# Other staging places, and other load times, for the four split operands of the first down group

## What is computed

```
h = x + rms_norm(mixer(...), n_mix_post)
f = square(relu(rms_norm(h, n_ffn_pre) @ w_up)) @ w_down      # 1024 -> 4096 -> 1024, fp32
y = h + rms_norm(f, n_ffn_post)
```

## Time and profile before

| | us |
|---|---|
| median of 3 runs | 1588.58 |
| the profiled execution | 1588.32 |
| its span | 1586.3 |
| PE busy in it | 1531.6 |
| DVE, POOL, ACT busy | 933.8, 710.3, 507.2 |

### The profile page before, as it was taken

One profiled execution on the slowest core, in us unless ns is written; L12 is line 12 of the kernel. 1 busy time (PEld: TensorE's weight loads), 2 busy tenths in 40 slices (PEclk: granted clock), 3 DMA queues, 4 the chain that ended last, 5 costly groups with the idle time before them and its releaser, 6 DMA issues.

```text
span 1586.3 us, 27880 instructions
## 1 busy us (share of the span) xinstructions
PE 1531.6 (97%) x10928; PEld 1515.1 (96%) x10928; DVE 933.8 (59%) x1202; ACT 507.2 (32%) x701; POOL 710.3 (45%) x508
## 2 busy tenths in 40 slices
PE   6999999999999999999999999999999799999995
PEld 5999999999999998999999999999999799999995
DVE  6899959764485235211152785776566557474746
ACT  4100000242240224100112566665556333232333
POOL 3344444442244222444448344554555355454555
PEclk9999999999999999999999999999999899999998
DMA  5211121113321232111143024566658576464634
GB/s 178 94 47 47 46 61 47 40 60 106 94 94 46 85 98 73 43 46 46 47 154 93 1 88 147 188 216 239 214 187 305 183 274 214 161 214 161 214 101 161
DMA packets 99034, 194.85 MB, mean 123 GB/s; under 512 B 7920, under 2 KB 19952, under 8 KB 97024
## 3 DMA queue, kind: packets, MB, share of 16 engines
q1 hardware_dynamic: 85008, 169.98, 31.9%
q10 hardware_dynamic: 13936, 23.60, 4.6%
HBM read 137.50 MB, written 56.05 MB: 122 GB/s over the span
## 4 chain that ended last, share of the span: by engine, by line
PE 53%; DVE 3%; ACT 1%; DMA 1%; POOL 1%; issue 1%; SPq 0%; POOLq 0%; DVEq 0%; ACTq 0%
PE ps L1018 37%; PE ps L672 13%; PE ps L931 3%; DMA hq_g<-hidden_scratch 1%; DVE tx_l L427 1%; ACT mix L1356 0%; ACT fx_h L1339 0%; SPq L489 0%; POOL h_res L617 0%; DVE hq_g L2135 0%; POOLq L96 0%; POOL fac L652 0%; DVE mix L1945 0%; DVE mix L1942 0%; DVE mix L1943 0%
## 5 line engine op out<-in xcount | busy, mean ns | idle before, releaser
L583 POOL TENSOR_TENSOR w_h<-raw,zero 128x512 fp32r<-128x512 f32 x130 | 143.2, 1101 | 503.4 <-PE ps L672 381.8
L1018 PE MATMUL ps<-tx_h,w_h 128*128 128x258 f32 x960 | 272.8, 284 | 12.9 <-POOL w_l L641 12.4
L1018 PE MATMUL ps<-tx_l,w_h 128*128 128x258 f32 x960 | 272.3, 284 | 0.0
L1018 PE MATMUL ps<-tx_h,w_l 128*128 128x258 f32 x960 | 272.1, 283 | 0.0
L641 POOL TENSOR_TENSOR w_l<-raw,w_h 128x512 fp32r<-128x512 f32 x120 | 180.0, 1503 | 162.8 <-ACT w_h L1411 162.1
L672 PE MATMUL ps<-xn_h,w_h 128*128 128x344 f32 x1128 | 247.8, 326 | 2.4 <-DVE xn_l L1635 1.4
L672 PE MATMUL ps<-xn_l,w_h 128*128 128x344 f32 x1128 | 241.7, 320 | 0.0
L672 PE MATMUL ps<-xn_h,w_l 128*128 128x344 f32 x1128 | 240.8, 319 | 0.0
L1018 PE MATMUL ps<-fx_h,w_h 128*128 128x258 f32 x720 | 204.1, 283 | 0.0
L1018 PE MATMUL ps<-fx_l,w_h 128*128 128x258 f32 x720 | 203.4, 282 | 0.0
L1018 PE MATMUL ps<-fx_h,w_l 128*128 128x258 f32 x720 | 203.2, 282 | 0.0
(11 more groups left out here) (287 smaller groups left out, 2598.5 us busy)
## 6 DMA issues: line engine op xcount, KB each, us to landing
raw<-wseq_dram SPq DMA_DIRECT2D x264, 256.0 KB, 2.7
quad_scratch<-quad_h SPq DMA_DIRECT2D x16, 774.0 KB, 3.6
tx_h<-quad_scratch SPq DMA_DIRECT2D x12, 1032.0 KB, 10.4
tx_l<-hidden_scratch SPq DMA_DIRECT2D x12, 1032.0 KB, 12.8
hidden_scratch<-hq_g SPq DMA_DIRECT2D x8, 1032.0 KB, 6.9
hq_g<-hidden_scratch SPq DMA_DIRECT2D x8, 1032.0 KB, 12.3
hidden_scratch<-stg_b SPq DMA_DIRECT2D x6, 1032.0 KB, 6.9
rope<-rope_dram ACTq DMA_DIRECT2D x2, 2064.0 KB, 7.9
```

The source lines that it names most:

```text
L583: pool.tensor_tensor(hi, raw[:, s, :], zero[:, 0:1].broadcast_to([P, SLOT]), ALU.add).then_inc(w_hi, 1)
L1018: out = pe.matmul(ps[:, 2 * n + s, 0:HC], RINGS[q % RING][wa][:, kk * P:(kk + 1) * P], OPS[x][xb][:, QK * kh + kk, at_:at_ + HC], start=(i ...
```

## The change

```diff
+        op0, _ = place("op0", [P, QK, HT], F32, a_C0)
...
-        def staged_h(k):
+        def staged_h(g, k):
+            if g == 0 and k < 2:
+                return op0[:] if k == 0 else hq_d[:, 4:8, :]
+            if g == 0:
+                k -= 2
             return (stg_a, stg_b)[k][:, 0:QK, HT:T] if k < 2 else hq_g[:, 4 * k - 8:4 * k - 4, :]
...
             def load_operand(g, k):
-                if g:
+                if g == 1 and k < 2:
+                    lo_made(sp, 0, k + 2)
+                elif g > 1:
                     lo_made(sp, g - 1, k)
-                sp.dma_start(staged_h(k), uscr[g, OP_SLOT[SPLIT[k]]]).then_inc(stg_ld[k], 16)
+                sp.dma_start(staged_h(g, k), uscr[g, OP_SLOT[SPLIT[k]]]).then_inc(stg_ld[k], 16)
...
+                if v in (UPV - 5, UPV - 4):
+                    for u in (QK - 2, QK - 1):
+                        stored(sp, u)
+                    if v == UPV - 4:
+                        sp.wait_ge(hs_sq, 2 * KT)
+                        sp.wait_ge(h_sp, 16 * len(H_STORE))
+                    load_operand(0, v - (UPV - 5))
                 if v == UPV - 2:
-                    stored(sp, UNITS - 4)
-                    quads_stored(sp, UNITS - 4)
-                    load_operand(0, 0)
-                    load_operand(0, 1)
+                    for u in (QK - 2, QK - 1, UNITS - 4):
+                        stored(sp, u)
+                        quads_stored(sp, u)
+                    load_operand(0, 2)
+                    load_operand(0, 3)
                 if v >= UPV - 1 and p == 3 and v + 1 < NV:
                     for i in range(2, 5):
                         load_quads(g + 1, i)
-                        if v == UPV - 1 and i != 3:
-                            stored(sp, UNITS - 3)
-                            quads_stored(sp, UNITS - 3)
-                            load_operand(0, 2 + i // 4)
...
                 if d >= 0 and p == 1 and g + 1 < GROUPS:
...
+                    if g == 0:
+                        stored(sp, UNITS - 3)
+                        quads_stored(sp, UNITS - 3)
                     for k in range(4):
                         load_operand(g + 1, k)
```

More of the change, by code:

```diff
@@ L1430, in staged_hi @@
                 act.wait_ge(pm, step_done(UPV + QK * g - 1, SPLIT[k]))
-                quad_hi(SPLIT[k], staged_h(k)).then_inc(c_hi, 1)
+                quad_hi(SPLIT[k], staged_h(g, k)).then_inc(c_hi, 1)
             def h_square(n):
@@ L2006, in staged_lo @@
                     dve.wait_ge(c_hi, 4 * g + k + 1)
-                    quad_lo(dve, SPLIT[k], staged_h(k), slice(2 * half, 2 * half + 2)).then_inc(c_lo, 1)
+                    quad_lo(dve, SPLIT[k], staged_h(g, k), slice(2 * half, 2 * half + 2)).then_inc(c_lo, 1)
             def h_add(n):
```

## The result

The changed kernel takes 1577.64 us (median of 5 runs, 1577.53 to 1581.27) against 1588.58 us before (5 runs, 1588.06 to 1594.04). The ratio is 0.9931, with a 95% interval of 0.9918 to 0.9944: 0.7% faster. Forecast were 1576.3 us and a range of 1575.2 to 1578.8.

A forecast was written before the change was run, and what follows sets the result against it. PE, busy 97% of the span, was taken as the bound. Profiled 1588.32 minus 12.29 gave 1576.03, plus 0.26 to the median: 1576.3 us, range 1575.2 to 1578.8; this path had 79% and its own range 1575.4 to 1577.2.

The forecast's parts named there:

- The bound, and the mechanism: PE bounds; at v=14 it idles 10.6 us because step 3's weight waits behind late k=3 in ACT's queue.
- (a): At v=14 ACT finds k=2 and k=3 loaded; copies start at 1232.10 and 1233.93, the weight's high part at 1235.76.
- (b): Step 3's weight is late next: PE waits 0.47 to 1.04 us, taking POOL's median of 1.46 us.
- other sum: POOL, contending with DVE, takes 1.85 us for step 3's weight; time 0.39 us more than forecast.
- The price of the hole: Step 3 took 5.22 us behind the hole against 2.87 at full clock; the low clock cost 2.35 us.
- ceiling of 12.94: Most that can be won, in us: step 3's old end at 1253.11 minus its end without the hole, 1240.17.
- (c): Gain 12.29 us; behind step 3 nothing else waits: operand i=4 lands near 1239.2, step 6 is covered by 1.7 us.
- first rival: Direct operand i=4 still lands at 1241.6, making step 4 0.8 us late: gain 11.5, time 1577.1 us; chance 10%.
- (d): One added 1032 KB load at v=9 and one at v=10 cost 0, at most 2.7 us each.
- (e): Moved waits at v=15 and copies from other SBUF places cost 0; places bounded at 0.1 us either way.
- Clock rivals: Remaining wait at step 3 drops the clock again (1578.6 us, 5%), or PE without rest gets less clock (3%).
- slower rival: Unbroken PE run behind 1240.8 us is throttled: clock 0.963 loses the gain, 0.95 gives 1593.4 us; chance 3%.

The follow-up runs named there:

- ACT-order experiment: Kernel before the change, loads and places unaltered; at v = 14 ACT makes high parts of weights 3, 4, 5 ahead of staged copy k = 3: 1581.5 us.
- late k = 3 experiment: Changed kernel, but only k = 2 (and k = 0) leaves the load burst; k = 3 is loaded last at v = 13: 1585.73 us.
- both weights first: Changed kernel with ACT making the high parts of step 3's and 4's weights ahead of staged copies k = 2 and 3: 1576.36 us.
- weight-between experiment: Changed kernel; ACT makes step 3's weight between both staged copies, DVE the second half of k = 2's low part after emptying step 2's banks: 1576.48 us.
- k = 2 late: Changed kernel, but only k = 3 (and k = 1) leaves the burst; k = 2 is loaded at v = 13 between direct operands 2 and 3: 1577.85 us.

## Why the prediction was right, step by step

- **The bound, and the mechanism** (the weight of step 3 behind k = 3 in ACT's queue): right. The ACT-order experiment removes the hole without touching a load; the late k = 3 experiment keeps it with k = 2 gone.
- **(a) k = 3 and k = 2 no longer awaited**: right. In the old profile's time (0.92 us less) the copies start at 1232.10 and 1233.94 and the weight's high part at 1235.75, against 1232.10, 1233.93 and 1235.76.
- **(b) What is late next**: the right wait, 0.28 us too short. POOL took 1.74 us here (1.75 in the other two profiles of the program), and I took the median of 1.46. It was inside the bounds (1.28 to 1.85), but DVE was busy beside it. In the rows at this point the one that starts second pays. In the changed kernel POOL starts at 1237.37, within DVE's half of k = 2's low part (1236.75 to 1237.97), and takes 1.74 instead of 1.28, while that half takes 1.22. With both weights first POOL ends at 1238.05 and DVE's second half, started at 1237.41, takes 1.73 instead of 1.23. The Trainium skill's rule (GPSIMD Engine Reference, Key points), by which I had the other sum, was the better guide: 1.85 is 0.11 us from what was measured, 1.46 is 0.28.
- **The price of the hole**: mis-sized by 0.32 us. I counted step 3 as 2.87 us from its start. It took 1242.34 - 1239.15 = 3.19 us at full clock. After each wait that I read at steps 3 and 4 (of 0.2 to 0.9 us, in six profiles) the step took 3.14 to 3.19 us up to the instructions that wait for it, some 0.3 us more than in an unbroken stream; I call this the refill. So of the 2.35 us that I put down to the clock, 0.3 were this and 2.03 the clock (from the start of step 3 to the last 48 matmuls: 308.08 us before, 306.05 after). The ceiling of 12.94 stands; what remains of it, as 12.94 - 11.69 = 1.25 us, is the wait of 0.93 with its refill, and the weight-between experiment got 1.17 of it back, which leaves 0.24 for the refill.
- **(c) The covers**: right. Operand i = 4 landed at 1239.84, 1238.9 in the old time (forecast 1239.2); steps 4 and 6 didn't wait. Its cover is one transfer: with one more ahead (k = 2 late) step 4 waits 0.2 us. So the first rival's mechanism exists, but it isn't the next limit of the changed kernel. Once the weight of step 3 is in time, what is late is DVE's copy of step 2's banks (both weights first), a wait that the prediction didn't name. The first weight of v = 15 landed at 1242.55, 1241.6 in the old time (forecast near 1242).
- **(d) The added loads cost nothing**: right, and with room: all four in one unit cost nothing either. PE's piece from the start of the MLP stretch to the end of v = 13 is 164.12 us for 1368 matmuls in the changed kernel and in the ACT-order experiment, which has the old loads.
- **(e) The moved waits and other places cost nothing**: right. ACT's two copies take 1.94 and 1.91 us from `stg_a` and `stg_b`, and behind step 3 PE waits for nothing in the loop but the 0.5 us near 1545 us that it waits before the change too.
- **Clock rivals**: no drop behind the remaining wait in any of the three profiles of the changed program (from step 3 to the last 48 matmuls they take 306.05, 306.02 and 306.06 us). The ground that I gave for it was weak, though: the wait behind the earlier trace rows is 1.8 us long, of which the window shows 1.5, and waits of this length do drop the clock in some executions (last section). PE ran 472 us without a rest in the weight-between version, and the clock reads 1.00 over all of it from 1070 to 1540 us. The slower rival has nothing for it.
- **The total**: 1577.64 against 1576.3. The profiled execution was forecast at 1576.03 and took 1577.55. Of these 1.5 us, 0.6 are the two sizes above (a gain of 11.69 instead of 12.29), and 0.9 is where it stood before the MLP, which the changed program's second profile doesn't repeat (its set: 1576.65). The path that I gave 79% had its own range, 1575.4 to 1577.2, and that was missed by 0.4. I had allowed half a microsecond of scatter, and one program's medians move by about one. That 1577.64 lies in the wide range up to 1578.8 is in part luck: its upper part was meant for a late i = 4 and a clock step, and neither came. It is also nearer to the first rival's 1577.1 than to the forecast, for reasons that aren't that rival's.

## What to carry to other kernels

When the wait chain ends in a transfer, ask which engine's queue stood behind it: the first work lost here was not the user of the late data but a weight that was queued behind it, and swapping the order gave half of the gain (6.3 of 11.7 us) without moving a byte. Price a hole in TensorE's work as its length, plus what the clock gives away behind it (2.0 us here), plus 0.2 to 0.3 us of refill. Where a change starts late in a long kernel, measure it from a common event just ahead of it; the whole-run median is blurred by things that it didn't touch.

## What the runs showed of the hardware beside this

Much of the scatter of whole runs arises before the MLP, from PE's early waits and from its clock behind them. In the profile of the late k = 3 experiment (1590.82 us, against its median of 1585.73) the clock reads 0.91 at 20 to 40 us and again at 940 to 960 us, where profiles of usual length read 1.00. First that profile, then the changed kernel's second:
```profile
20.00:40.00 20.00, 16.55 (x85) 14.83 (x83) 16.09 (x18) 9.33 (x16) 8.82 (x5) 0.91 0.13 37
940.00:960.00 20.00, 18.20 (x128) 17.99 (x128) 16.96 (x13) 8.76 (x12) 9.60 (x6) 0.91 0.44 150
```
```profile
20.00:40.00 20.00, 19.24 (x108) 17.04 (x107) 16.92 (x19) 10.89 (x20) 8.77 (x5) 1.00 0.10 37
940.00:960.00 20.00, 18.18 (x148) 17.98 (x148) 15.07 (x14) 7.54 (x12) 9.32 (x7) 1.00 0.52 180
```
The MLP of that profile starts at 1069.82 us, 5.3 us later than the other's. By 643 us it is already 3.75 us late (646.43 against 642.68), and the larger part of that isn't the clock: at 20 to 40 us PE waits 3.4 us for DVE's `xn_l` there instead of 0.8, since DVE takes 9.69 us for eight of them instead of 6.81. The low clock (0.67 from 28 to 32 us) stands behind the longer wait, of 2.7 us. The profile of the weight-between experiment (1579.16 us) shows the same, with 3.4 us of waits and 0.59; in the other eight PE waits at most 1.1 us at a time for these operands, and the clock reads 1.00. Why DVE takes longer isn't shown.

In the second of these stretches lies the wait near 948 us from which I argued that a short wait leaves the clock at 1.00; it does in most executions, and not in all. It is 1.8 us long in seven of the ten profiles, and behind it the clock stays at 1.00 in six and reads 0.79 and 0.78 (952 to 960 us) in one. A wait of 1.9 us near 910 us is in all ten: behind it the clock reads 0.57 over a window of 4 us in three (the changed kernel's first, both weights first, weight between) and 1.00 in seven. Behind the 0.9 us at step 3 it read 1.00 in all five profiles that have it. So behind a single wait of less than 2 us the clock fell in some executions and not in others, and the program text up to there is the same in all. The 2.9 us wait of the ACT-order experiment had the drop (0.75 and 0.69) behind it; whether the one of 1.7 us some 6 us ahead had a part in it wasn't tried.
